# VectorE's step in the joint attention stream: scaling first, then the stores, then the logits of new scores

## What is computed

```python
        d = pb[None, None, :, None] - tok
        bsel = jnp.moveaxis(table_g[gi, t5_bucket(d)], -1, 2)
        sq = jnp.einsum('bqghd,bgqsd->bghqs', qb, kg).astype(jnp.float32) * scale + bsel
        ps = masked_softmax(sq, (d >= 0)[:, :, None])
        return jnp.einsum('bghqs,bgqsd->bqghd', ps.astype(vg.dtype), vg)
```

## Time and profile before

| what | before |
| --- | --- |
| median of 3 runs | 2598.74 us (2597.78 to 2602.55) |
| the profiled execution | 2593.48 us, its span 2591.5 us |
| mean granted TensorE clock | 0.942 of full speed |
| TensorE matmul busy | 2311.3 us, 89% of the span |
| TensorE weight loads busy | 2092.9 us, 81% |
| VectorE busy | 1090.8 us, 42% |
| ScalarE busy | 695.3 us, 27% |
| GpSimd busy | 416.3 us, 16% |

### The profile page before, as it was taken

How to read it: one execution, slowest core, us unless ns; L and a number is a source line. 1 busy time by engine, 2 the same in 40 slices (tenths; PEclk the granted TensorE clock), 3 DMA queues, 4 the chain that set the end, 5 groups by cost and what they waited for, 6 DMA issues and landing times. The chain is left out here.

```text
span 2591.5 us, 41142 instructions
## 1 busy us (share of the span) xinstructions
PE 2311.3 (89%) x15977; PEld 2092.9 (81%) x15977; DVE 1090.8 (42%) x2461; ACT 695.3 (27%) x1391; POOL 416.3 (16%) x374
## 2 busy tenths in 40 slices
PE   8999675876888887999899969899999999999995
PEld 7799664774555556999798956699999999999995
DVE  2212355125566573122217203427755555553335
ACT  3210153103555563011135002435211111121122
POOL 0000011320322211212111100011212212222220
PEclk9999887788999998999899989999999999999997
DMA  3211203877433423111131043512111111111212
GB/s 135 96 48 49 15 1 104 282 255 273 165 133 104 134 84 104 49 49 42 62 107 33 17 146 131 199 49 96 46 49 49 41 49 49 38 40 49 108 41 75
DMA packets 114348, 233.22 MB, mean 90 GB/s; under 512 B 23442, under 2 KB 76339, under 8 KB 110723
## 3 DMA queue, kind: packets, MB, share of 16 engines
q1 hardware_dynamic: 85034, 177.94, 20.9%
q0 software_dynamic: 10368, 28.33, 3.3%
q10 hardware_dynamic: 18754, 24.35, 2.7%
HBM read 207.28 MB, written 27.47 MB: 91 GB/s over the span
## 5 line engine op out<-in xcount | busy, mean ns | idle before, releaser
L88 PE MATMUL psum<-x_half_high,ff_half 128*128 128x352 f32 x3240 | 792.2, 324 | 13.9 <-DVE h_again_low L69 9.0
L88 PEld LDWEIGHTS psum<-x_half_high,ff_half 128*128 128x128 f32 x3240 | 568.6, 189 | 15.2 <-DVE ff_half L69 9.2
L88 PE MATMUL psum<-h_again_low,ff_half 128*128 128x352 f32 x1176 | 379.0, 322 | 0.0
L69 POOL TENSOR_TENSOR ff_half<-ring,ff_half 128x1024 fp32r<-128x1024 f32 (+2 forms) x85 | 177.2, 2086 | 760.9 <-ACT ff_half L3048 760.9
L88 PEld LDWEIGHTS psum<-h_again_low,ff_half 128*128 128x128 f32 x1176 | 222.8, 189 | 0.0
L88 PE MATMUL psum<-merged_high,oq_half 128*128 128x352 f32 x768 | 190.0, 328 | 13.0 <-DVE oq_half L69 12.8
L3048 ACT ACTIVATE ff_half<-ring 128x1024 fp32r<-128x1024 f32 (+2 forms) x88 | 78.0, 888 | 433.5 <-PE psum L88 407.3
L88 PE MATMUL psum<-mid_low,ff_half 128*128 128x352 f32 x516 | 167.0, 324 | 0.0
L88 PEld LDWEIGHTS psum<-merged_high,oq_half 128*128 128x128 f32 x768 | 136.4, 192 | 13.5 <-DVE oq_half L69 13.1
L1706 PE MATMUL psum<-consts,na_p 128*128 128x128 f32 x528 | 86.5, 303 | 50.5 <-DVE na_p L1987 41.2
L1706 PEld LDWEIGHTS psum<-consts,na_p 128*128 128x128 f32 x528 | 62.0, 152 | 83.5 <-DVE na_p L1987 58.9
(11 more groups left out here) (551 smaller groups left out, 4232.6 us busy)
## 6 DMA issues: line engine op xcount, KB each, us to landing
na_kv<-in_pool SPq DMA_DIRECT2D x128, 128.0 KB, 3.5
na_kv<-in_pool POOLq DMA_DIRECT2D x128, 128.0 KB, 4.0
sab_kv<-in_pool SPq DMA_DIRECT2D x96, 128.0 KB, 4.4
mg_w<-in_w_merge SPq DMA_DIRECT2D x16, 768.0 KB, 4.4
sab_kv<-in_pool POOLq DMA_DIRECT2D x88, 128.0 KB, 4.7
ring<-in_f_wu SPq DMA_DIRECT2D x22, 512.0 KB, 3.7
ring<-in_f_wg SPq DMA_DIRECT2D x22, 512.0 KB, 3.7
sab_kv<-in_pool ACTq DMA_DIRECT2D x72, 128.0 KB, 4.6
```

What stands on the lines that cost most here:

```text
L69: return engine.tensor_tensor(low, x, high.bitcast(F32), ALU.subtract)
L88: ins = nc.tensor.matmul(out, w[a], x[b], start=first and n == 0, stop=last and n == 2)
```

## The change

VectorE's step in the joint stream gets another order: `factors(n + 2)` first, then `store(n - 1)`, then `logits(n + 3)`. The exception for PAGES items goes away, as their logits are last in every step now. The other engines' loops, all instructions and all semaphores stay as they are.

```diff
             for n in range(-3, U + 1):
+                if 0 <= n + 2 < U:
+                    factors(n + 2)
                 if n >= 1:
                     store(n - 1)
-                paged = n + 3 < U and items[n + 3][0] == PAGES
-                if n + 3 < U and not paged:
-                    logits(n + 3)
-                if 0 <= n + 2 < U:
-                    factors(n + 2)
-                if paged:
+                if n + 3 < U:
                     logits(n + 3)
```

## The result

| | before | changed |
| --- | --- | --- |
| median of 4 runs each | 2600.64 us (2597.78 to 2603.69) | 2644.48 us (2642.80 to 2645.22) |
| the profiled execution, its span | 2593.48 us, 2591.5 us | 2642.80 us, 2640.8 us |
| mean granted TensorE clock | 0.942 | 0.934 |

The changed kernel takes 1.0176 times as long (95% interval 1.0159 to 1.0192), 43.8 us more. 2641 us had been forecast.

The account below looks back on a forecast made before the run. The stage was taken as bound by hand-overs, with no engine full. Terms of +22.0, +15.9 and +4.6 us summed to +42.5, profiled 2593.5 to 2636, median about 2641 us; range 2617 to 2659, or to 2668 with most of the clock rival.

Parts of the forecast that it names:

- L, E, F, L, E, F become one serial chain: Logits, exponential, scaling of each item run serially over VectorE and ScalarE; 2.87 us a step at 256 columns; chance 0.78.
- Part 1: Query tiles 0 to 3, stretches without pages: 24.4 us serially against 18.9, in four head pairs, +22.0 us.
- Part 2: The 14 tiles of 640 columns and more with a page item: excess 22.5 us, saving 6.6, so +15.9 us.
- the term of the clock: TensorE's granted clock may fall as it idles more: taken as nothing, other end +18 us and up to 10 more.
- the two ends of the prediction: Bounds for the clock's cost: tile 4 kept full speed through 1.75 us of waiting, tile 7's clock fell after 1.90.
- Part 3: The last two tiles, without a page: copies of the last SEL tile start at 975.5 instead of 970.91, +4.6 us.
- The signs: In the stage: wait for L1812 over 80 us, TensorE's scaling wait shrinks, VectorE's scores wait halves, next stage some 40 later.
- One sign of being half wrong: The granted clock of the stage falls well below its 0.94; the other sign was only stretches without pages growing.
- TensorE as the bound: Rival at the transposes (L1706): their 41.2 us of waiting is saved, the kernel gets faster, 2557 us; chance 0.05.
- Trading places: Rival: VectorE's 61.1 us of waiting for scores absorbs all new waiting; 2599 us, up to 2604; chance 0.04.
- The falling clock: Rival: TensorE's clock falls too, on top of the serial chain: +60 to +70 us, 2659 to 2669; chance 0.13.
- The whole upper end of 18 + 10 us: Most the clock could add: 1.3 us for each of 14 page tiles, +18 us, and up to 10 in narrow stretches.

Follow-up runs that it names:

- the quartered exponential: SEL and SLIDE exponentials over a quarter of their columns, mask constant -1000: in the changed kernel 2589.94 us (0.9977), in the kernel before 2596.40 us (1.0001).
- the second session: The changed kernel run again, unaltered, beside three experiments on one chip, against the kernel before: 2647.31 us, ratio 1.0198.

## Why the prediction was right, and where its terms were off

**The cause.** "L, E, F, L, E, F become one serial chain over VectorE and ScalarE, with VectorE idle through each E" is what happens. The wait of L1983 for L1812 is 104.0 us (over 80 forecast), and the quartered exponential, worth 54 us in the changed order and nothing in the old one, shows that it is the exponential that holds the chain. That the median came out 3.5 us from the forecast is in part luck: Part 1 too high and Part 2 too low made up for each other, and the same kernel lost 51.4 us in the second session.

**Part 1**, forecast +22.0 us, measured +19.0. The stretch of the second pair is 23.85 us against 24.4; the step of 256 columns 2.78 against 2.87. The steps had been taken 0.4 us too long in all, and three stores delay the next logits by 0.2 us each where four had been counted for 1.3; against that, VectorE waits 0.53 us for TensorE's scores in two places, which the sum had at nothing. The four pairs add 4.7, 5.2, 4.0 and 5.1 us where 5.5 each was taken.

**Part 2**, forecast +15.9, measured +23.2. This is the step that failed in its size. The copies start within 0.1 us of the end of E(SLIDE), 755.50, as forecast. But tile 4 costs 2.3 to 2.6 us where 1.36 less 0.3 was taken, and tile 5 2.6 to 4.0 (1.7 in the last pair) where 2.43 less 0.3 was. Tile 6 costs 0.2 to -0.8 and tile 7 0.7 to 1.9. What was mis-sized is the term of the clock, "I take nothing". In tile 4 the way from copies to page logits rose from 3.15 to 4.58 us at a granted clock of 0.50, just the missing 1.4 us, and by 1.5 or 1.6 in the other pairs. Four such tiles are some 6 us of the 7.3 that Part 2 is over its forecast. In tile 5 that way is no longer than it was (3.78 us for 3.81), in tile 7 the clock had been low already, 5.19 us in the earlier trace rows and 5.45 now, and in tile 6 of the second and third pairs the clock was low before and stayed at 1.00 in this execution, which is why that tile got cheaper. In the changed kernel of the second session tile 6 lost it too.

I did not work out the new wait either: E(SLIDE) starts later than the first two pieces of the transposes, so TensorE's wait for the copies had to grow, to 3.14 us in tile 4. But the two ends of the prediction, full speed behind 1.75 us and a low clock behind 1.90, are not a matter of length. In the trace of before, in tile 6 of the second pair, TensorE waits 1.77 us (to 769.75), and in 771 to 773 us the clock is 0.50.

**Part 3**, forecast +4.6, measured +4.6, and by the way forecast: from L(SEL, tile 6) to the copies of the last SEL tile it takes 27.7 us (990.08 to 1017.82), 27.8 had been added up.

**The store.** The prediction counted it inside the chain (1.3 us a narrow stretch, 0.3 in the tail, and the combination's 5.4 us), and never priced it by itself. By the medians it is 16 to 20 us of the loss, which leaving the store ahead of the scaling would have avoided.

**The sum** of 42.5 us stands against 47.0 in the profiled stage and 43.8 between the medians.

**The signs.** VectorE's wait for scores fell from 61.1 to 15.4 us, TensorE's for the scaling from 41.2 to 20.2. The stage's successor starts some 47 us later (40 forecast), and the rest of the kernel is 2.3 us longer. One sign of being half wrong came true as well, a granted clock of the stage well below its 0.94: it is 0.89.

**The rivals.** TensorE as the bound (2557 us) is refuted: it gained 21 us at the wait named, and the wait for the copies, at the same line, took 41 back. Its condition was right, an exponential short enough: at a quarter of it the new order is no slower (0.9977). And the gap was real. Moving TensorE's own values into it gave 18 us (2578.07), and with the pages' scores ahead as well 41 us (2556.59). That this is the rival's number is chance, as a good part of it comes from the waits for the pages' scores. The rule of the Trainium skill (Perfetto Trace Analysis, Optimization Strategy), to make what the busiest engine waits for start sooner, gave a kernel 1.76% slower where the producer of that work had to wait itself. Trading places forecast no loss; there are 43.8 us, and both halves lose. The falling clock, with its 0.13, is true in part: 0.94 went to 0.89 in the stage, and it fell in the wide tiles that I had named, for some 6 us in the profiled execution of the result and probably more in that of the second session, whose stage was 8 us longer at a lower clock. The whole upper end of 18 + 10 us was not reached. That repeated gaps make each burst start slow (the Trainium skill, TensorE: Matmul & The Clock Gate, HAM oscillation) agrees with the 0.50 behind 3.14 us of waiting. Not every burst behind such a wait starts slow, though: 2.54 us left the clock at 1.00, and 2.99 us too.

**What stays open.** What decides whether the clock falls behind a wait of 1.8 to 3.1 us; how much of the store's 16 to 20 us and of the quartered exponential's 54 us is the clock; and the order of values and scores of a page.

## What to carry to other kernels

On a queue that runs strictly in order, an operation that waits for what the instruction just ahead of it set off turns two overlapping engines into one chain: keep at least one item's worth of other work between the two, and put what is already due (stores, combinations) ahead of a wait. Before moving a producer forward for the sake of a gap on the busiest engine, see whether that engine has work of its own, ready, behind the wait; that order was worth 41 us here, and the other cost 44. To see which engine a step hangs on, shorten the suspected operation in both orders and compare. And where the clock moves, compare the stage in the traces as well as the medians: 9.5 us of median could not be pinned to the edited stage here.

## What the runs showed that was not expected

When GpSimd copies the strip of position bias while VectorE scales, the scaling takes about twice as long. The timeline of the changed kernel, in tile 5 of the first head pair:

```profile
676.07 2.73 DVE L1987 TENSOR_SCALAR na_p<-na_p,na_rs,branch_gates 128x640 f32<-128x640 f32 x2
676.27 1.05 POOL L1578 COPY na_wstrip<-na_strip 128x1024 f32<-128x1024 f32 x1
677.28 0.64 POOL L1579 TENSOR_TENSOR na_wstrip<-na_strip,consts 128x256 f32<-128x256 f32 x1
```

A pair of this form takes 1.14 us elsewhere (at 918.74, for one). The excess is 1.59 us, and GpSimd's two instructions last 676.27 to 677.92, 1.65 us. That they exclude each other instead of sharing is what the Trainium skill says of the port pair of VectorE and GpSimd (SBUF — State Buffer, "SBUF: two separate sides"); the two lengths agree with it. It is so in the second head pair too, where GpSimd came first: its two instructions last from 778.16 to 779.82, and VectorE's pair from 778.42 to 780.69, 2.27 us. In both cases the pair ends 0.87 to 0.88 us behind GpSimd's last. Before the change GpSimd's copy ran at 668.90, where VectorE did logits, and cost nothing; here it cost next to nothing too, as VectorE waited 0.54 us for the page's scores behind it.
